# Attention in pairs of steps, and the low pass of two heads' logits in the two halves of TensorE's rows

## The reference, cut to what matters

```
logits = einsum('btngd,btsnd->btngs', q, k) * HEAD_DIM ** -0.5
logits = where(valid, logits, -inf)
p = softmax(logits, axis=-1)
o = einsum('btngs,btsnd->btngd', p, v)
```

## Time and profile before

| | |
|---|---|
| runs | 1313.05, 1315.21, 1312.52 us |
| profiled execution | 1312.2 us, span of its records 1310.4 us |
| granted TensorE clock, mean of the span | 0.988 |
| PE busy | 97% of the span |
| chain of waits, share by engine | PE 70%, DVE 13%, ACT 5% |
| attention | from the first L3190 at 342.46 us to the last L3204 at 488.45 us |

### The profile page before, as it was taken

How to read it: one execution, slowest core, us unless ns; L and a number is a source line. 1 busy time by engine, 2 the same in 40 slices (tenths; PEclk the granted TensorE clock), 3 DMA queues, 4 the chain that set the end, 5 groups by cost and what they waited for, 6 DMA issues and landing times.

```text
span 1310.4 us, 25268 instructions
## 1 busy us (share of the span) xinstructions
PE 1273.1 (97%) x9537; PEld 1155.5 (88%) x9537; DVE 859.0 (66%) x1586; ACT 672.1 (51%) x1151; POOL 732.5 (56%) x473
## 2 busy tenths in 40 slices
PE   6899999989899999999999999999999999999998
PEld 4677999877666656999999999999999999999998
DVE  6777889889677738667983454555545563644595
ACT  5647888969776766455352343333334336211115
POOL 0242448990332102457577877888878857765620
PEclk8899999999899989999999999999999999999999
DMA  9722116432101126555321343433435168999633
GB/s 354 271 69 74 50 37 214 154 129 81 52 14 34 45 76 215 170 164 155 109 103 46 117 162 131 163 129 130 162 139 184 67 259 300 324 342 340 246 130 131
DMA packets 127274, 198.86 MB, mean 152 GB/s; under 512 B 16839, under 2 KB 100111, under 8 KB 116656
## 3 DMA queue, kind: packets, MB, share of 16 engines
q1 hardware_dynamic: 127008, 193.01, 42.7%
q10 hardware_dynamic: 144, 4.23, 0.8%
HBM read 144.07 MB, written 53.18 MB: 151 GB/s over the span
## 4 chain that ended last, share of the span: by engine, by line
PE 70%; DVE 13%; ACT 5%; DVEq 4%; ACTq 2%; issue 2%; SPq 2%; DMA 1%; POOL 0%; POOLq 0%
PE ps L3505 30%; PE ps L3525 15%; DVE junk L2071 3%; PE ps L3204 3%; ACT junk L1355 3%; PE ps L3190 3%; ACTq L1357 2%; PE ps L3369 2%; PE ps L3371 2%; PE ps L3370 2%; PE ps L3179 2%; DMA ada_shift<-in_ada_w 1%; PE ps L3180 1%; DVEq L2621 1%; PE ps L3322 1%
## 5 line engine op out<-in xcount | busy, mean ns | idle before, releaser
L3525 PE MATMUL ps<-input,down_H 128*128 128x258 f32 x1120 | 180.7, 283 | 1.5 <-DVE acc L2769 1.5
L3525 PEld LDWEIGHTS ps<-input,down_H 128*128 128x128 f32 x1120 | 154.5, 190 | 2.3 <-issue 1.3
L3505 PE MATMUL ps<-comb,opH 128*128 128x258 f32 x960 | 154.4, 283 | 0.0
L1171 POOL TENSOR_TENSOR opL<-wsum,opH 128x512 fp32r<-128x512 f32 x80 | 123.8, 1557 | 36.3 <-ACT opH L1688 32.9
L1688 ACT CAST opH<-wsum 128x512 fp32r<-128x512 f32 x80 | 49.6, 621 | 167.7 <-PE ps L3505 114.5
L3505 PEld LDWEIGHTS ps<-comb,opH 128*128 128x128 f32 x960 | 132.7, 190 | 0.0
L3505 PE MATMUL ps<-h2H,opH 128*128 128x258 f32 x640 | 129.0, 283 | 0.3 <-DVE h2L L2626 0.3
L3505 PE MATMUL ps<-h2H,opL 128*128 128x258 f32 x640 | 129.0, 283 | 0.0
L3505 PE MATMUL ps<-h2L,opH 128*128 128x258 f32 x640 | 128.6, 282 | 0.0
L1014 POOL TENSOR_TENSOR wL<-wraw,wH 128x1024 fp32r<-128x1024 f32 x28 | 70.1, 2505 | 91.6 <-ACT wH L1348 91.3
L2769 DVE TENSOR_TENSOR acc<-ps,acc 128x516 f32<-128x516 f32 x112 | 76.6, 694 | 62.4 <-PE ps L3525 61.9
(11 more groups left out here) (528 smaller groups left out, 3546.4 us busy)
## 6 DMA issues: line engine op xcount, KB each, us to landing
down_inputs<-staged SPq DMA_DIRECT2D x35, 1032.0 KB, 4.3
input<-down_inputs SPq DMA_DIRECT2D x35, 1032.0 KB, 7.1
adb<-in_ada_w SPq DMA_DIRECT2D x8, 2048.0 KB, 8.0
wraw<-in_w_out SPq DMA_DIRECT2D x24, 512.0 KB, 4.4
raw<-in_w_gate SPq DMA_DIRECT2D x10, 1024.0 KB, 6.6
raw<-in_w_up SPq DMA_DIRECT2D x10, 1024.0 KB, 5.0
down_block<-in_w_down SPq DMA_DIRECT2D x5, 2048.0 KB, 10.9
x_feature_major<-x0T ACTq DMA_DIRECT2D x1, 4128.0 KB, 15.0
```

Of the source, the lines that this page charges most:

```text
L1171: pool.tensor_tensor(opL[g % OPS][:], operand(v, p), opH[g % OPS][:].bitcast(F32), ALU.subtract).then_inc(s_wL, 1)
L3505: ins = mm(ps[:, sum_bank(v, p) + h, 0:HC], weight[s][:, k, :], token[:, k, h * HC:(h + 1) * HC], start=begins, stop=ends, skip_group_chec ...
L3525: ins = mm(ps[:, 2 * m + h, 0:HC], weight[:, f, cc], tok[:, f, part, h * HC:(h + 1) * HC], start=(f == 0 and weight is hi and part == 0), ...
```

## The change

Three things are done.

1. The stack of an odd head is turned round: low part first, then high part (`stack_high`, `stack_low`). After the transpose the high query of an even head lies on rows 0 to 63 and that of an odd head on rows 64 to 127.
2. `logits(g)` now makes heads g and g + 1 together. The first pass is as before, for one head and then the other. The second pass multiplies only the high query by the low keys, 64 rows for each head: the even head in the upper half of the array's rows, the odd one in the lower half, one instruction right after the other, into different banks. The product low x low falls away. Both heads are released together.
3. The loops on TensorE and ScalarE and the list of banks run by pairs of steps: query transposes, two heads' logits, two `transposed`, then the `mixed` of the pair before. `decode_masks` and `group_sums` are placed to fit.

```diff
-                rows = qk[:, i, 0:NH * HD].rearrange("p (h d) -> p h d", h=NH)
-                pool.tensor_copy(stk[:, :, 0, :].bitcast(F32R), rows)
+                pool.tensor_copy(stack_high().bitcast(F32R), query_rows(i))
                 pool.drain()
-                pool.tensor_tensor(stk[:, :, 1, :].bitcast(F32R), rows, stk[:, :, 0, :], ALU.subtract).then_inc(s_ql, 1)
+                pool.tensor_tensor(stack_low().bitcast(F32R), query_rows(i), stack_high(), ALU.subtract).then_inc(s_ql, 1)
...
 # ScalarE
-                for step in range(max(GRP + 1, i + 1)):
-                    if step <= i:
-                        probs_out(n, step)
-                    if step == Q_STEP and new + 1 < NG:
+                for even in range(0, max(GRP + 1, i + 1), 2):
+                    if even == Q_STEP and new + 1 < NG:
                         q_evac(new + 1)
-                    if (n, step) == (KEYS_N, KEYS_STEP):
+                    if new < NG and even == Q_STEP:
+                        exponential(GRP * new + 1)
+                    for step in (even, even + 1):
+                        if step <= i:
+                            probs_out(n, step)
+                    if (n, even) == (KEYS_N, KEYS_STEP):
                         last_keys_high()
-                    if new < NG and 1 <= step <= GRP:
-                        exponential(GRP * new + step - 1)
+                    if new < NG and even <= GRP:
+                        exponential(GRP * new + (0, 2, 3)[even // 2])
...
 # TensorE, logits(g)
-                if g >= 2:
-                    pe.wait_ge(s_lm, g - 1)
-                for n0, w in halves(P * (tile_of(n) + 1)):
-                    dst = ps[:, 2 * (g % 2) + n0 // 512, 0:w]
-                    q = qT[:, g % NLG, :]
-                    mm(dst, q, kT[:, n % 2, 0, n0:n0 + w], start=True, stop=False)
-                    ins = mm(dst, q, kT[:, n % 2, 1, n0:n0 + w], start=False, stop=True)
-                ins.then_inc(s_lg, 1)
+                keys = halves(P * (tile_of(n) + 1))
+                for e in range(2):
+                    if g >= 2:
+                        pe.wait_ge(s_lm, g - 1 + e)
+                    for n0, w in keys:
+                        mm(ps[:, 2 * e + n0 // 512, 0:w], qT[:, (g + e) % NLG, :], kT[:, n % 2, 0, n0:n0 + w],
+                           start=True, stop=False)
+                for n0, w in keys:
+                    for e in range(2):
+                        half = slice(e * HD, (e + 1) * HD)
+                        ins = mm(ps[:, 2 * e + n0 // 512, 0:w], qT[half, (g + e) % NLG, :],
+                                 kT[half, n % 2, 1, n0:n0 + w], start=False, stop=True)
+                        if (n0, w) == keys[-1]:
+                            ins.then_inc(s_lg, 1)
...
 # TensorE, the loop
-                for step in range(max(GRP, i + 1)):
-                    if step <= i:
-                        transposed(n, step)
-                        if len(behind) == 2:
-                            mixed(*behind.pop(0))
-                        behind.append((n, step))
...
+                for even in range(0, max(GRP, i + 1), 2):
+                    if even == Q_STEP and new + 1 < NG:
+                        q_transposed(new + 1)
+                    if new < NG and even < GRP:
+                        logits(GRP * new + even)
+                    turned = [(n, step) for step in (even, even + 1) if step <= i]
+                    for rows in turned:
+                        transposed(*rows)
...
+                    if turned:
+                        for rows in behind:
+                            mixed(*rows)
+                        behind = turned
```

More of the change, by code:

```diff
@@ L153, in bank_items @@
     for n in range(NG):
[L154 to L157, removed]
+        for even in range(0, max(GRP, tile_of(n) + 1), 2):
+            if even == Q_STEP and n + AHEAD + 1 < NG:
                 order.append(("q", n + AHEAD + 1, 0))
-            if (n, step) == (KEYS_N, KEYS_STEP):
+            order += [("rows", n, step) for step in (even, even + 1) if step <= tile_of(n)]
+            if (n, even) == (KEYS_N, KEYS_STEP):
                 order.append(("keys", 0, 0))
@@ L435, in summed, with stack_high, stack_low, query_rows @@
             return ps[:, sum_bank(v, p):sum_bank(v, p) + 2, 0:HC]
+        def stack_high():
+            return stk[:].rearrange("p (k e) r d -> p k (e r) d", e=2)[:, :, 0::3, :]
+        def stack_low():
+            return stk[:].rearrange("p (k e) r d -> p k (e r) d", e=2)[:, :, 1:3, :]
+        def query_rows(i):
+            return qk[:, i, 0:NH * HD].rearrange("p (k e d) -> p k e d", e=2, d=HD)
         def two(ap):
@@ L1463, in q_high @@
                     act.wait_ge(s_bt, q_item(1) + 1)
-                nc.scalar.copy(stk[:, :, 0, :].bitcast(F32R),
-                               qk[:, i, 0:NH * HD].rearrange("p (h d) -> p h d", h=NH)).then_inc(s_qs, 1)
+                nc.scalar.copy(stack_high().bitcast(F32R), query_rows(i)).then_inc(s_qs, 1)
             def q_evac(n):
@@ L1519, in _ @@
                 i, new = tile_of(n), n + AHEAD
-                for step in range(max(GRP + 1, i + 1)):
-                    if step <= i:
-                        probs_out(n, step)
-                    if step == Q_STEP and new + 1 < NG:
+                for even in range(0, max(GRP + 1, i + 1), 2):
+                    if even == Q_STEP and new + 1 < NG:
                         q_evac(new + 1)
-                    if (n, step) == (KEYS_N, KEYS_STEP):
-                        last_keys_high()
-                    if new < NG and 1 <= step <= GRP:
-                        exponential(GRP * new + step - 1)
[L1529 to L1532, removed]
+                    if new < NG and even == Q_STEP:
[3 more added lines that the diff above has]
+                            probs_out(n, step)
+                    if (n, even) == (KEYS_N, KEYS_STEP):
+                        last_keys_high()
+                    if new < NG and even <= GRP:
+                        exponential(GRP * new + (0, 2, 3)[even // 2])
+                    if n == NG - 2:
+                        act.wait_ge(s_lh, even // 2 + 1)
+                        lru_square(even // 2)
+                    if n == NG - 1:
                         act.wait_ge(s_hd, NG - 2)
-                        if step // 2 == LT - 1:
+                        if even // 2 == LT - 1:
                             act.wait_ge(s_hd, NG - 1)
-                        heads_square(step // 2, 0, NTT - 1)
-                    if n == NG - 1 and step == ROOT_STEP:
+                        heads_square(even // 2, 0, NTT - 1)
+                    if n == NG - 1 and even == ROOT_STEP:
                         group_root(0)
@@ L3236, in _ @@
             pe.wait_ge(s_lev, NU_LRU)
-            for g in range(AHEAD * GRP):
+            for g in range(0, AHEAD * GRP, 2):
                 logits(g)
@@ L3289, in _ @@
                 i, new = tile_of(n), n + AHEAD
-                for step in range(max(GRP, i + 1)):
-                    if step <= i:
-                        transposed(n, step)
-                        if len(behind) == 2:
-                            mixed(*behind.pop(0))
-                        behind.append((n, step))
-                    if (n, step) == (NG - 2, 3):
-                        decode_queries()
[L3298 to L3302, removed]
+                for even in range(0, max(GRP, i + 1), 2):
[6 more added lines that the diff above has]
+                        transposed(*rows)
+                    if (n, even) == (KEYS_N, KEYS_STEP):
+                        last_keys_turned()
+                    if turned:
+                        for rows in behind:
+                            mixed(*rows)
+                        behind = turned
+                    if (n, even) == (NG - 2, 2):
+                        decode_queries()
+                    if (n, even) == (NG - 1, 2):
+                        decode_masks(0, 3)
+                    if (n, even) == (NG - 1, 4):
                         group_sums(0, 0, 4)
-                    if (n, step) == (NG - 1, 6):
+                    if (n, even) == (NG - 1, 6):
                         group_sums(0, 4, NTT)
[L3306 to L3311, removed]
             def turned_pages(b):
```

4 lines of the change are left out of this document (1 added, 3 removed).

## The result

The change is no gain. Twelve runs of the changed kernel have a median of 1314.03 us (1312.22 to 1317.13), twelve of the kernel before on the same chip 1312.34 us (1309.41 to 1315.21): ratio 1.0018, 95% interval 1.0011 to 1.0026. That is 2.4 us slower, inside the 0.2% that was to count as none. Forecast were 1305.5 us and a range of 1302 to 1313.5; the measured median lies above it. The profiled execution of the changed kernel has a span of 1312.1 us, the one before 1310.4.

What follows compares the result with a forecast made beforehand. TensorE, busy 97% of the span, was taken as the bound. Gains of 7.8 + 0.3 = 8.1, then + 0.5 - 0.9 + 0.3 - 0.5 = 7.5 us off 1312.2, plus 0.85 to the median: 1305.5 us, range 1302 to 1313.5.

Steps and rivals of the forecast that it cites:

- rival 1: Low passes on TensorE: row halves run side by side only in part, 1.3 passes, 2.3 us lost, 1308 us; chance 0.10.
- rival 3: Low passes on TensorE: the halves run one behind the other, the 7.8 us fall away, 1313 us; chance 0.13.
- rival 4: Between low passes on TensorE: weight loads laid bare, 6.4 us on top of no overlap, 1320 us; chance 0.09.
- Logits before the loop: Prologue: the next pair waits for both masks, last three pairs 0.4 to 0.5 us later each, 1.4 us in all.
- the 1.2 us of groups 0 to 3: Early loop groups with one or two blocks of keys: changes of form on TensorE lose 1.2 us together.
- My own sign of being wrong: The prediction is wrong if the low pass shows no overlap, or PE waits more than 5 us in the loop.
- a loose end: Clock at half speed in stretches around attention: 6.8 us cost some 3.4; one stretch more or less is 1.7 us.
- The 7.8 us of the low pass: Logits of 28 pairs of heads: one pass saved per pair if row halves run side by side, 7.8 us gained.
- all changes of form (+0.3): Array form changes on TensorE in both loops: 22.4 us before, 22.1 after, a gain of 0.3 us.
- Groups 4 to 15 with their deductions: Later loop groups: 9.3 us gain, less 0.9 for mask waits, plus 0.3 for decode masks, less 0.5 for small waits.
- Rival 2: Attention loop, groups 8 to 13: VectorE becomes the bound through masks and scans, 4 us lost, 1309.5 us; chance 0.12.
- Behind attention: Work after attention: it starts earlier too, with some 9 us of slack for the output weights, so the gain passes.

Runs made afterwards that it cites:

- the complement: The changed kernel with row halves only for logits of groups 0 to 5 and full low passes from group 6 on: 1314.64 us, ratio 1.0018.
- the last-named fast kernel: Kernel before with pairs of steps from group 6, logits head by head, no row halves, scan of group 8 ahead of the low keys: 1302.53 us, ratio 0.9924.
- the swap: VectorE's scan of group 8 put ahead of the low keys, against the kernel combining the winning parts (1304.61 us): 1301.79 us, ratio 0.9929 to the kernel before.
- the fastest kernel: Kernel before with pairs of steps from group 6, row halves from group 12, scan of group 8 ahead of the low keys: 1301.79 us, ratio 0.9929.
- the joint release: The changed kernel with the low pass on all 128 rows, pair order and release of both heads together kept: 1306.98 us, ratio 0.9967 to the kernel before.

## Why the prediction was wrong

**The sizes of TensorE's operations were right.** Halves side by side, 0.095 us for a change of form, 1.79 us for a pair at w = 1024; group 14, which has no logits left to make, won 1.64 us (10.19 to 8.55) where 1.6 was forecast. Rivals 1, 3 and 4 fall with them. In rival 4 the Trainium skill ("TensorE: Matmul & The Clock Gate", what overlaps and what doesn't) stood against the earlier trace rows. The four low passes of 444.50 and the changes around them took 0.66 us, the prediction's 0.46 and 0.20, so no load is laid bare between them, and the row decides. The 3.07x for four row tiles, which rival 1 took from the Trainium skill (the same page, measured speedup vs the span model), was no measure for two halves: four half passes took the time of two, 2.0x.

**The step that failed is the early one.** "Logits before the loop" (1.4 us) and the 1.2 us of groups 0 to 3 were to come to a net loss of 0.7 us, the rest hidden behind waits for GpSimd's stack. From the same small projection to the first work of group 4, where both programs have the same work behind them, it was 7.7 to 10.1:

```profile
335.33:360.20 24.87, 21.73 (x129) 16.61 (x129) 13.22 (x59) 20.30 (x64) 9.72 (x11) 0.86 0.24 67
338.20:371.12 32.92, 26.32 (x130) 17.35 (x129) 14.12 (x61) 21.77 (x66) 10.17 (x11) 0.74 0.23 65
```

The first line is of the kernel before, the second of the changed one; their other profiles took 25.18 and 34.95 us. The waits for masks that I priced at 1.4 us in the prologue came, as 0.49 + 0.48 + 0.39. What I left out was the same wait in the groups 0 to 3 (0.62, 0.61, 0.76 and 0.74 us) and the one for the copy of the queries (0.72): I followed one chain, GpSimd's, and took its stack for what the groups wait on anyway (PE waited 0.6 us on it, before 1.4). The pair order in short groups puts the second pair of one group, the queries' transposes and the first pair of the next behind each other with little between. Up to group 4 idle time of PE was 6.6 and 6.35 us against 3.1 and 3.7. So 2.7 to 3.5 us of the loss are idle time; 4.1 to 7.0 are the slow clock, of which the next paragraph tells. Undoing the order in six groups (with its row halves), or only moving the transposes ahead, gives most of the time back. My own sign of being wrong, more than 5 us of waits in the loop, showed too: 6.6 us, 2.4 of them behind the scan.

**The clock was named as a loose end and priced at one stretch.** I wrote 1.7 us for one more or less and looked for it late. It came early: 17.1 and 23.9 us at half clock in the two profiles, 23.9 in the complement, against 6.8 in each profile of the kernel before. By busy time at half clock that is 4.1 us in the one and (20.56 - 6.62) / 2 = 7.0 in the other. The runs put the whole cost of the row halves at 6.7 us, some 2 of which the rows give to their changes of form. That the row halves bring the slow clock is shown by two programs with them in the early groups in that order, one of them in two profiles, by two that have full passes there (6.8 and 10.3 us), and by the granted clock of all their runs; how passes on half of the rows lead to it is not.

**The 7.8 us of the low pass were not a net gain of the row halves.** The sum took the low pass (+7.8) and all changes of form (+0.3) as they stood, and I wrote that this part pays for itself. Had I cost the two edits apart, with the same rows, I would have seen it: the row halves add two changes for each of 28 pairs, 28 x (0.200 + 0.152) = 9.9 us, and save 7.8; the pairs of steps alone save the rest, some 10 us by the rows. The traces bear the count out: 138 changes of form in the changed kernel's attention, 84 with full low passes, 146 before. In time row halves are worth nothing measurable late, and minus 6.7 us early. Pairs of steps are worth 4.5 us in all groups, and from group 6 on 7 to 8 (10.0 of the last-named fast kernel, 0.9924, less 1.6 to 3.0 for the swap).

**What held.** Groups 4 to 15 with their deductions (9.3 - 0.9 + 0.3 - 0.5) made 8.2 us. From the first work of group 4 to the end the changed kernel took 941.0 and 941.6 us, the third and fourth profile of the one before 947.1 each: 5.5 to 6.1 of the 8.2. The wait on the mask behind the scan was 2.1 + 0.26 us where I had 2.2; that the clock would be at half for 3.4 us behind it, 1.7 us more, I had not, and that is most of what is missing. Of ten profiles with this wait nine have half clock right behind it, the one with logits head by head has none. Rival 2, VectorE as the bound, has that one place in the late groups, which the swap of two operations removes. Behind attention the gain passes, as forecast: the fastest kernel's last product is 10.6 us earlier than in the first profile of the kernel before (478.1 against 488.7), its span 10.4 shorter.

**The balance.** 5.5 to 6.1 won late, 7.7 to 10.1 lost early: 2 to 4 us slower by the profiles, 2.4 by the runs. The first profile of the kernel before does not show this sum, since it began the attention early and then had two stretches of half clock behind 477 us (the second profile has one, the third and fourth none): its 840.3 us from the first transposes of group 15 to the end stand against 838.5, 837.3 and 837.3. I had one profile and took those two stretches for the kernel's.

Open stays why 64-row passes with waits between them go with a low clock for so long. Open stays also why logits head by head from pairs of steps (0.9966) gain no more than with the joint release (0.9967), though PE waited less on the masks in the early groups (2.2 us against 3.9). Their profiles differ in the clock both ways, 10.2 us against 6.8 at half clock early, none against 3.4 late, and one profile of each can't say which of it is typical.

## What to carry to other kernels

Price every edit of a change by itself, with its own changes of form, before summing: a part that "pays for itself" may be one that costs and one that gains. Where an order is changed for a loop of growing steps, walk through the shortest steps first, on each engine's queue, and ask what stands between two operations that reuse a buffer; a hybrid, old order for the short steps and new for the long, took the gain here. Look at the granted clock behind each longer wait, too: in nine of ten profiles the late wait of 2.1 us was followed by half clock that cost 1.7 us or more on top. And take more than one profile of the kernel before when the stake is half a per cent: where the half clock falls moves by execution.

## What the runs showed of the hardware

Two passes on 64 rows each, one per half, start 0.003 to 0.004 us apart (0 to 0.008 over all 48 such couples of the changed kernel) and end within 0.012 us of each other: one pass in time. In the early groups, where passes on half rows stood with waits of 0.4 to 0.8 us between them, the granted clock was at half (1.2 of 2.4 GHz) for up to 23.9 us, while the same order with full passes had 6.8 to 10.3 us, and the same row halves with transposes ahead of the first pair 10.3. Behind one wait of 2.1 us at full clock, nine of ten profiles have 3.4 to 6.8 us of half clock. The start of the attention varies from 335.3 to 339.8 us over four profiles of one program, and the half clock behind 470 us is there in two stretches, one, or none; the earliest start went with a span of 1310.4 us, the latest with 1312.1.
